# Order of rounding, drains and small statistics at four section changes, and whole 2 MB ring slots for projections with 4 or 8 k tiles

## The chip, the cores and the metric

The kernel runs on one core of a Trainium2 chip. The metric is the device time of one execution in microseconds. The five engines are TensorE (PE), VectorE (DVE), ScalarE (ACT), GpSimd (POOL) and SyncE (SP); each works through its own instructions in program order and waits at semaphores for the others.

## What is computed

The input is one sequence of 256 tokens with 2048 columns, fp32. It goes through an even layer (a gated causal convolution of 31 taps with layer norm and a pointwise projection, beside block attention of 8 heads), an odd layer (latent attention of 16 heads with an index score that keeps 64 keys per query), a mixer (gated delta rule and a short convolution), cross attention to 256 memory rows, and a feed-forward part with a 3-tap convolution. Each is a residual with an RMS norm in front. Nearly all time goes to projections. The change touches these parts of the reference:

```python
z = _rmsnorm(x, norm_g) @ w_in                      # even and odd layer
...
ya = _conformer_conv(...) * silu(a_gate)            # ends with y @ w_pw + b_pw      (e_pw)
x + jnp.concatenate([ya, yb], -1) @ w_out           #                                (e_out)
...
cq, ckv, ik, iw, gate = _split_cols(z, [512, 256, 64, 16, 2048])   # (o_small, o_gate0, o_gate1)
cq, ckv = _rmsnorm(cq, q_norm), _rmsnorm(ckv, kv_norm)
q  = cq @ w_qb                                      #                                (o_q)
iq = cq @ w_iq                                      #                                (o_iq)
ik = _layernorm(ik, ik_g, ik_b)
```

## The kernel before

**Tiling.** Every projection is a `Seg` (a section): `units` blocks of weights, `kt` k tiles of 128 rows. A narrow unit is 128 output columns for all k tiles, and its result is a [128, 256] tile in one of two PSUM banks. A wide unit (`e_out`, `o_out`, `f_down` and others) is a quarter of the k tiles for 512 output columns; four of them end a group of columns in PSUM for both halves of the tokens. Units are numbered through the whole kernel by `n0 + j`.

**Three products.** Weights and activations are each split in two fp32r parts, `hi` (the rounded value) and `lo` (the rest), and PE adds hi times hi, lo times hi and hi times lo. For each unit, ACT copies the weights of the ring slot to `w_hi` (`split`, L1090, wide L1087), DVE subtracts to get `w_lo` (L1604, wide L1600), PE multiplies (L604 and L605 for the paired sections, L607 to L609 for the others, L645 to L647 for the wide ones). The four buffers `whi`/`wlo` are used in turn, so a unit can be split once the unit four before it is done on PE. The activations lie in `h_cat`, written in rounds of four tiles: ACT writes the high part (`h_round`, L1267) and DVE the low part (`h_rest`, L1774).

**The ring.** SP loads weights into `RING = 2` slots of 2 MB. A chunk of the ring is two units, whatever `kt` is: 2 MB with 16 k tiles, 1 MB for `e_pw` with 8, 0.5 MB for `o_iq` and `o_q` with 4. The DMA for chunk c waits until every unit of chunk c - 2 is split.

**Order on ACT and DVE.** Behind the last matmul of a unit, ACT drains its PSUM bank (`drain`, for example L1104, L1124, L1138) and DVE does what follows (`post`: for paired sections L1637 adds the other half of the bank, then convolution taps or a product). Both lag three units behind the splits (`LAG = 3`). PE may write a bank again when the unit two before it is drained, or summed where the section is paired. `seg` runs a section: split unit j, drain or post unit j - 3. `section(name)` stands between two sections: it finishes all drains (or posts) of the section that ends and then splits four units of the next one. Inside `seg` a callback (`also` on PE, `late` on ACT) puts smaller work beside the units: `key_beside` in `o_gate0` (layer norm of the index key, transposes of the latent rows), `index_beside` in `o_gate1` (index scores of 16 heads).

**The statistics of `cq`, `ckv` and `ik`.** After `o_small` ACT squares `cq` and `ckv` (L1337, L1339), PE sums them over partitions with a matrix of ones (L749 to L752) before it begins `o_gate0`, ACT takes the roots (L1341, L1342) and DVE scales (L1892 to L1901).

**The feed-forward part.** It runs in three pieces, `f_up0` to `f_up2` (up projection, 3-tap convolution, SiLU, product on GpSimd at L553 to L557 into `act_cat`) and `f_down0` to `f_down2` (wide). On ACT the move from up to down has no `section`; on DVE it has `section(down.name)`.

Of the kernel before, what the change touches and what calls it, by code (L numbers as in the profile page):

```python
# [195 lines left out]
def build(nc, a, out):  # L196
# [149 lines left out]
    def p_tile(a_):  # L346
# [8 lines left out]
             "ht_hi", "ht_ready", "hhi_ready", "h_ready", "x_normed", "gain1_loaded", "gain_out_loaded",  # L355
# [41 lines left out]
    def chunk_src(g, c, k):  # L397

        cols2 = 2 * P
# [51 lines left out]
    def _(sp):  # L451
        sp.dma_start(x[:, 0, :], a["x"][0, 0:P]).then_inc(sem["x_loaded0"], 16)

        def load(g, i, b, looped):
# [15 lines left out]
            for cols, src in srcs:  # L470
                sp.dma_start(ring[slot][:, 0:g.kt, cols], src).then_inc(loaded[slot], 16)

        for g in order:
# [4 lines left out]
            for b in range(2):  # L478
                load(g, 0, b, False)
# [95 lines left out]
    def _(pe):  # L575
        mm = nc.tensor.matmul

        def unit(g, j, n, i=None, rhs=None, tiles_ready=None, norm=None):
# [13 lines left out]
            for k in range(g.kt):  # L592
# [21 lines left out]
        def seg(name, tiles_ready=None, rhs=None, also=None, norm=None):  # L614
# [3 lines left out]
            for j in range(g.units if straight else 4):  # L618
                unit(g, j, g.n0 + j, None, rhs, tiles_ready if j == 0 else None, norm if j == 0 else None)
# [130 lines left out]
        for t in range(CKT):  # L750
            mm(ps[3][:, 0:T], ones[:], osq[:, QT + t, :], start=(t == 0), stop=(t == CKT - 1))
        mm(ps[4][:, 0:T], ones[0:IDX_DIM, :], ik[0:IDX_DIM, :], start=True, stop=True).then_inc(sem["cq_stat"], 1)  # L752
# [31 lines left out]
        seg("o_gate1", also=index_beside)  # L784
# [279 lines left out]
    def _(act):  # L1064
# [10 lines left out]
        def split(g, j, n, i=None):  # L1075

            slot, m, kn = n % WHL, width(g, j), (n if i is None else n + 4 * i)
            c = g.c0 + (n - g.n0) // 2
# [10 lines left out]
            u0 = ((n - g.n0) % 2) * P  # L1089
            af(whi[slot][:, 0:g.kt, 0:m], ring[c % RING][:, 0:g.kt, u0:u0 + m], ACT.Copy).then_inc(sem["hi_ready"], 1)  # L1090
# [234 lines left out]
        section("e_out")  # L1325
# [10 lines left out]
        section("o_gate0")  # L1336
# [247 lines left out]
    def _(dve):  # L1584
# [7 lines left out]
        def split(g, j, n, i=None):  # L1592

            slot, m, kn = n % WHL, width(g, j), (n if i is None else n + 4 * i)
            c = g.c0 + (n - g.n0) // 2
# [7 lines left out]
            u0 = ((n - g.n0) % 2) * P  # L1603
            tt(wlo[slot][:, 0:g.kt, 0:m], ring[c % RING][:, 0:g.kt, u0:u0 + m],  # L1604
# [275 lines left out]
        section("e_out")  # L1880
# [8 lines left out]
        section("o_gate0")  # L1889
        dve.wait_ge(sem["cq_stat"], 1)  # L1890
        dve.wait_ge(*emptied(S["o_small"], 8))
        ch.link(nc.vector.tensor_scalar(ikt[:], ps[4][:, 0:T], 1.0 / IDX_DIM, None, ALU.mult))  # L1892
        ch.link(tt(ik[:], ik[:], ikt[:], ALU.subtract))
        tt(ikt[:], ik[:], ik[:], ALU.mult).then_inc(sem["ik_sq"], 1)
        dve.wait_ge(sem["cq_std"], 1)
        ch.link(nc.vector.reciprocal(orq[:], orq[:]))
        for t in range(CKT):
            ins = stt(ckv[:, t, :], ckv[:, t, :], col("kv_norm", t), orq[:, 1, :], ALU.mult, ALU.mult)
        ins.then_inc(sem["ckv_normed"], 1)
        for t in range(QT):  # L1900
            ins = stt(cq[:, t, :], cq[:, t, :], col("q_norm", t), orq[:, 0, :], ALU.mult, ALU.mult)  # L1901
        ins.then_inc(sem["cq_normed"], 1)
# [35 lines left out]
        section("o_q")  # L1938
# [291 lines left out]
```

## Time and profile before

| | |
|---|---|
| median of 3 runs | 2778.83 us (2774.16 to 2781.66) |
| profiled execution | 2779.45 us, span 2777.7 us, mean granted clock 0.966 |
| PE busy | 2553.9 us, 92% |
| DVE, ACT, GpSimd busy | 60%, 43%, 6% |
| DMA | 422.95 MB, mean 152 GB/s |

A line of the timeline gives the start in us, the duration in us, the engine, the line of code, the operation, output and inputs with shapes, and how many instructions of the same kind were merged (x4). In square brackets stands the idle time of the engine just before it, and what ended it. The granted clock is 1.00 at 2.4 GHz and 0.50 at 1.2 GHz; a number between them is a mean over a stretch with both.

### The profile page before, as it was taken

What the parts mean: (1) busy time and instruction counts of PE and PEld (TensorE: products, weight loads), DVE (VectorE), ACT (ScalarE), POOL (GpSimd) and SP (SyncE); (2) the same over time, 40 slices, a digit from 0 to 9 for tenths busy, and PEclk for the clock granted to TensorE, in tenths of its full rate; (3) what the DMA queues carried; (4) which work ended last, traced back from release to release, by engine and by line L of the source; (5) the groups of instructions that cost most, each with busy time, mean ns of one, the idle gap of its engine ahead of it and who ended that gap; (6) DMA issues with size and microseconds to landing.
All of it is one profiled execution on the core that took longest, in us unless ns stands there. A gap on an engine that the chain in (4) does not pass through costs nothing.

```text
span 2777.7 us, 36975 instructions
## 1 busy us (share of the span) xinstructions
PE 2553.9 (92%) x14778; PEld 2235.9 (80%) x14778; DVE 1664.3 (60%) x1948; ACT 1190.7 (43%) x1400; POOL 159.8 (6%) x136
## 2 busy tenths in 40 slices
PE   5999889988889999999886998998999999999998
PEld 5878877888777788988875887996788788878886
DVE  4799745534654577486446545443577647765764
ACT  5333754533454554543224535433455434433433
POOL 0000000000110010000000000000012202220220
PEclk9999999999999999999998999998999999999999
DMA  5544525444341555554005454543555555546544
GB/s 193 175 153 168 166 92 182 155 137 149 96 141 54 182 165 170 176 163 147 1 1 182 159 174 153 180 145 105 175 182 181 177 187 186 190 168 201 187 134 159
DMA packets 356310, 422.95 MB, mean 152 GB/s; under 512 B 14667, under 2 KB 293978, under 8 KB 355418
## 3 DMA queue, kind: packets, MB, share of 16 engines
q1 hardware_dynamic: 352848, 411.32, 45.4%
q0 software_dynamic: 2160, 8.40, 0.9%
q8 instruction: 93, 1.52, 0.2%
q10 hardware_dynamic: 1178, 1.45, 0.1%
q14 instruction: 31, 0.25, 0.0%
HBM read 419.05 MB, written 2.10 MB: 152 GB/s over the span
## 4 chain that ended last, share of the span: by engine, by line
PE 82%; DVE 13%; ACT 3%; issue 1%; DMA 1%; ACTq 0%; DVEq 0%
PE ps L604 24%; PE ps L605 12%; PE ps L645 7%; PE ps L646 7%; PE ps L647 7%; DVE conv L1809 4%; PE ps L607 4%; PE ps L608 4%; PE ps L609 4%; PE ps L846 3%; DVE w_lo L1604 3%; DVE w_lo L1600 2%; PE ps L602 1%; PE ps L601 1%; PE ps L600 1%; PE ps L667 1%
## 5 line engine op out<-in xcount | busy, mean ns | idle before, releaser
L604 PE MATMUL ps<-h_cat,w_hi 128*128 128x512 f32 x3200 | 1144.8, 402 | 34.1 <-DVE h_cat L1774 14.1
L605 PE MATMUL ps<-h_cat,w_lo 128*128 128x256 f32 x3200 | 901.5, 282 | 0.0
L1604 DVE TENSOR_TENSOR w_lo<-ring,w_hi 128x2048 fp32r<-128x2048 f32 (+2 forms) x298 | 628.2, 2112 | 355.2 <-ACT w_hi L1090 352.5
L604 PEld LDWEIGHTS ps<-h_cat,w_hi 128*128 128x128 f32 x3200 | 604.7, 189 | 191.3 <-DVE w_lo L1604 15.8
L605 PEld LDWEIGHTS ps<-h_cat,w_lo 128*128 128x128 f32 x3200 | 608.3, 190 | 2.0 <-issue 1.9
L1090 ACT ACTIVATE w_hi<-ring 128x2048 fp32r<-128x2048 f32 (+2 forms) x298 | 525.3, 1768 | 130.6 <-PE ps L647 64.1
L1600 DVE TENSOR_TENSOR w_lo<-ring,w_hi 128x2048 fp32r<-128x2048 f32 (+1 forms) x120 | 272.0, 2283 | 232.0 <-ACT w_hi L1087 232.0
L1087 ACT ACTIVATE w_hi<-ring 128x2048 fp32r<-128x2048 f32 (+1 forms) x120 | 221.1, 1855 | 325.2 <-PE ps L647 251.4
L607 PE MATMUL ps<-h_cat,w_hi 128*128 128x256 f32 (+2 forms) x928 | 267.8, 289 | 10.8 <-DVE w_lo L1604 10.1
L608 PE MATMUL ps<-h_cat,w_hi 128*128 128x256 f32 (+2 forms) x928 | 263.9, 284 | 0.0
L645 PE MATMUL ps<-w_hi,h_cat 128*128 128x512 f32 x576 | 228.9, 397 | 38.0 <-DVE h_cat L1774 33.4
L609 PE MATMUL ps<-h_cat,w_lo 128*128 128x256 f32 (+2 forms) x928 | 263.7, 284 | 0.0
L1104 ACT ACTIVATE stage<-ps 128x256 f32<-128x256 f32 x144 | 55.4, 385 | 430.4 <-PE ps L605 430.4
L646 PE MATMUL ps<-w_lo,h_cat 128*128 128x512 f32 x576 | 227.9, 396 | 0.0
L647 PE MATMUL ps<-w_hi,h_cat 128*128 128x512 f32 x576 | 227.5, 395 | 0.0
L607 PEld LDWEIGHTS ps<-h_cat,w_hi 128*128 128x128 f32 (+2 forms) x928 | 174.8, 188 | 16.3 <-DVE w_lo L1604 10.9
L608 PEld LDWEIGHTS ps<-h_cat,w_hi 128*128 128x128 f32 (+2 forms) x928 | 174.9, 189 | 1.3
L609 PEld LDWEIGHTS ps<-h_cat,w_lo 128*128 128x128 f32 (+2 forms) x928 | 174.8, 188 | 1.2
L645 PEld LDWEIGHTS ps<-w_hi,h_cat 128*128 128x128 f32 x576 | 110.6, 192 | 63.1 <-issue 34.9
L645 PE MATMUL ps<-w_hi,act_cat 128*128 128x512 f32 x352 | 139.6, 397 | 13.2 <-DVE w_lo L1600 13.2
L1637 DVE TENSOR_TENSOR stage<-stage,ps 128x256 f32<-128x256 f32 x144 | 60.4, 419 | 134.9 <-ACT stage L1104 134.3
L646 PE MATMUL ps<-w_lo,act_cat 128*128 128x512 f32 x352 | 138.8, 394 | 0.0
(382 smaller groups left out, 2976.5 us busy)
## 6 DMA issues: line engine op xcount, KB each, us to landing
ring<-in_w_ffn_up SPq DMA_DIRECT2D x44, 2048.0 KB, 8.0
ring<-in_even_w_in SPq DMA_DIRECT2D x28, 2048.0 KB, 8.0
ring<-in_w_mix_in SPq DMA_DIRECT2D x28, 2048.0 KB, 8.3
ring<-in_w_ffn_down SPq DMA_DIRECT2D x16, 2048.0 KB, 8.1
ring<-in_odd_w_in SPq DMA_DIRECT2D x11, 2048.0 KB, 8.4
ring<-in_even_w_out SPq DMA_DIRECT2D x8, 2048.0 KB, 8.1
ring<-in_odd_w_out SPq DMA_DIRECT2D x8, 2048.0 KB, 8.5
ring<-in_w_mix_out SPq DMA_DIRECT2D x8, 2048.0 KB, 8.1
```

The lines of the kernel that those rows point to most:

```text
L604: mm(o[:, 0:2 * T], whi[slot][:, k, :], flat(cat[:, k]), start=first, stop=False)
L605: ins = mm(o[:, T:2 * T], wlo[slot][:, k, :], cat[:, k, 0, :], start=False, stop=end)
L607: mm(o[:m, 0:T], whi[slot][:, k, 0:m], cat[:, k, 0, :], start=first, stop=False)
L608: mm(o[:m, 0:T], whi[slot][:, k, 0:m], cat[:, k, 1, :], start=False, stop=False)
L609: ins = mm(o[:m, 0:T], wlo[slot][:, k, 0:m], cat[:, k, 0, :], start=False, stop=end)
L645: mm(o[:], cat[:, k, 0, toks], hi, start=first, stop=False)
L646: mm(o[:], cat[:, k, 0, toks], lo, start=False, stop=False)
L647: ins = mm(o[:], cat[:, k, 1, toks], hi, start=False, stop=end)
L1087: af(flat(whi[slot])[:, 0:size], flat(ring[c % RING])[:, u0:u0 + size], ACT.Copy).then_inc(sem["hi_ready"], 1)
L1090: af(whi[slot][:, 0:g.kt, 0:m], ring[c % RING][:, 0:g.kt, u0:u0 + m], ACT.Copy).then_inc(sem["hi_ready"], 1)
L1600: tt(flat(wlo[slot])[:, 0:size], flat(ring[c % RING])[:, u0:u0 + size], flat(whi[slot])[:, 0:size].bitcast(F32), ALU.subtract).then_inc(se ...
L1604: tt(wlo[slot][:, 0:g.kt, 0:m], ring[c % RING][:, 0:g.kt, u0:u0 + m], whi[slot][:, 0:g.kt, 0:m].bitcast(F32), ALU.subtract).then_inc(sem[" ...
```

## The change

1. `per_chunk` replaces the fixed two units of a chunk: 4 for `e_pw`, 8 for `o_iq` and `o_q`, so that every chunk is 2 MB. `e_pw` and `o_q` have two chunks and `o_iq` one. ACT and DVE write these sections out unit by unit instead of looping.
2. `e_pw` to `e_out`: ACT and DVE split one unit of `e_out`, then finish the drains and posts of `e_pw`, then run the rounds of `ya` and `qe`; the further units of `e_out` are split inside `wide_seg`.
3. `o_small` to `o_gate0`: ACT splits two units ahead of the last drains of `o_small`. The statistics on PE run behind unit 0 of `o_gate0`, the roots on ACT and the scaling on DVE at j = 2; the variance of the key on PE moves from j = 1 to j = 2 and the transposes from j = 3 to j = 4.
4. `o_gate1` to `o_q`: a new semaphore `tiles_read` is raised when the last unit of `o_gate1` has issued its k tile 3. ACT splits two units, drains up to two units before the end, splits a third, waits for `tiles_read`, rounds `cq` into `h_cat`, and then drains the rest. DVE splits three units instead of four.
5. `f_up` to `f_down`: DVE's `section(down.name)` is dropped, so the splits of `f_down` and the last posts of `f_up` alternate.

```diff
+        self.per_chunk = 2 if wide else max(2, 2 * KT // kt)
...
-        g.chunks = (g.units + 1) // 2
+        g.chunks = (g.units + g.per_chunk - 1) // g.per_chunk
...
+    def chunk(slot, g):
+
+        n = g.per_chunk * P
+        return flat(ring[slot])[:, 0:g.kt * n].rearrange("p (k n) -> p k n", n=n)
...
-        ends[c] = g.n0 + min(2 * j + 2, g.units)
+        ends[c] = g.n0 + min(g.per_chunk * (j + 1), g.units)
...
+                if read is not None and k == QT - 1:
+                    ins.then_inc(sem[read], 1)
...
-        pe.wait_ge(sem["cq_sq"], 1)
-        for t in range(QT):
-            mm(ps[2][:, 0:T], ones[:], osq[:, t, :], start=(t == 0), stop=(t == QT - 1))
...
         def key_beside(j):
-            if j == 1:
+            if j == 0:
+                pe.wait_ge(sem["cq_sq"], 1)
+                for t in range(QT):
+                    mm(ps[2][:, 0:T], ones[:], osq[:, t, :], start=(t == 0), stop=(t == QT - 1))
...
+            if j == 2:
                 pe.wait_ge(sem["ik_sq"], 1)
...
-            if j == 3:
+            if j == 4:
                 pe.wait_ge(sem["ckv_normed"], 1)
...
-        seg("o_gate1", also=index_beside)
+        seg("o_gate1", also=index_beside, read="tiles_read")
```

The same on ACT:

```diff
-        section("e_out")
+        split_to(S["e_out"].n0 + 1)
+        drain_to(S["e_out"].n0)
         ya_round(1)
...
-        section("o_gate0")
+        split_to(S["o_gate0"].n0 + 2)
+        drain_to(S["o_gate0"].n0)
         af(osq[:, 0:QT], cq[:], ACT.Square)
...
-        act.wait_ge(sem["cq_stat"], 1)
-        af(orq[:, 0, :], ps[2][:, 0:T], ACT.Sqrt, bias=eps[:], scale=1.0 / Q_LORA)
-        af(orq[:, 1, :], ps[3][:, 0:T], ACT.Sqrt, bias=eps[:], scale=1.0 / KV_LORA).then_inc(sem["cq_std"], 1)
         def key_beside(i, b):
+            if 4 * i + b == 2:
+                act.wait_ge(sem["cq_stat"], 1)
+                af(orq[:, 0, :], ps[2][:, 0:T], ACT.Sqrt, bias=eps[:], scale=1.0 / Q_LORA)
+                af(orq[:, 1, :], ps[3][:, 0:T], ACT.Sqrt, bias=eps[:], scale=1.0 / KV_LORA).then_inc(sem["cq_std"], 1)
...
-        section("o_q")
-        act.wait_ge(sem["acc_ready"], S["o_gate1"].n0 + 8)
+        split_to(S["o_q"].n0 + 2)
+        drain_to(S["o_q"].n0 - 2)
+        split_to(S["o_q"].n0 + 3)
+        act.wait_ge(sem["tiles_read"], 1)
         h_round(H_GROUPS["cq_again"], 1, lambda q: cq[:], lambda q: None)
+        drain_to(S["o_q"].n0)
```

And on DVE, where the scaling of `cq`, `ckv` and `ik` (L1890 to L1902) also moves into `key_beside` at j = 2:

```diff
-        section("e_out")
+        split_to(S["e_out"].n0 + 1)
+        post_to(S["e_out"].n0)
...
-        section("o_q")
+        section("o_q", 3)
...
             seg(f"f_up{p}", links=8)
-            section(down.name)
```

## Rows read from the trace of the kernel before

**Rows 1.** The page, busy time of each engine, its share of the span, instructions.
```profile
PE 2553.9 (92%) x14778; PEld 2235.9 (80%) x14778; DVE 1664.3 (60%) x1948; ACT 1190.7 (43%) x1400; POOL 159.8 (6%) x136
```

**Rows 2.** Waits of PE: us in total, how many times, the longest.
```profile
PE ps L645 <- DVE w_lo L1600: 17.7, 4, 4.6
...
PE ps L604 <- DVE h_cat L1940: 3.8, 1, 3.8
```

**Rows 3.** Timeline of ACT, DVE and PE where `e_pw` ends and `e_out` begins.
```profile
443.02 7.30 ACT L1087 ACTIVATE w_hi<-ring 128x2048 fp32r<-128x2048 f32 x4
...
451.17 2.00 ACT L1267 ACTIVATE h_cat<-qe 128x1024 fp32r<-128x1024 f32 x2
...
444.95 8.90 DVE L1600 TENSOR_TENSOR w_lo<-ring,w_hi 128x2048 fp32r<-128x2048 f32 x4 [0.85 <-ACT w_hi L1087]
...
447.30 0.80 PE L645 MATMUL ps<-w_hi,h_cat 128*128 128x512 f32 x1 [4.60 <-DVE w_lo L1600]
...
455.69 0.39 PE L645 MATMUL ps<-w_hi,h_cat 128*128 128x512 f32 x1
```

**Rows 4.** Timeline where `o_small` ends; L731 is an earlier sum at full clock.
```profile
591.56 7.29 ACT L1090 ACTIVATE w_hi<-ring 128x2048 fp32r<-128x2048 f32 x4
...
600.37 3.52 PE L749 MATMUL ps<-osq,ones 128*128 128x256 f32 x8 [9.13 <-ACT osq L1339]
...
605.32 0.39 PE L607 MATMUL ps<-h_cat,w_hi 128*128 128x256 f32 x1
...
384.89 3.61 PE L731 MATMUL ps<-conv,ones 128*128 128x256 f32 x16
...
617.53 1.28 ACT L1347 ACT_TABLE_LOAD   x1
618.83 0.48 ACT L1347 ACTIVATE rstd<-ps,eps 128x256 f32<-128x256 f32 x1
```

**Rows 5.** Timeline of SP, ACT and PE where `o_iq` ends and `o_gate1` begins.
```profile
658.04 29.55 SPq L471 DMA_DIRECT2D ring<-in_odd_w_in  x4
...
667.41 1.91 ACT L1090 ACTIVATE w_hi<-ring 128x2048 fp32r<-128x2048 f32 x1 [6.40 <-DMA ring<-in_odd_w_in]
...
672.12 0.76 PE L604 MATMUL ps<-cq_cat,w_hi 128*128 128x512 f32 x1 [8.59 <-DVE iq L1637]
...
680.81 1.14 PE L778 MATMUL ps<-ik,iq 64*128 64x256 f32 x8
```

**Rows 6.** Timeline of DVE and ACT from the start of `o_q` to `o_out`.
```profile
730.99 2.50 DVE L1604 TENSOR_TENSOR w_lo<-ring,w_hi 128x512 fp32r<-128x512 f32 x4 [11.42 <-ACT w_hi L1090]
...
734.64 3.83 DVE L1927 SCALAR_TENSOR_TENSOR isum<-relu,iwt,isum 128x256 f32<-128x256 f32 x8
...
775.43 3.71 ACT L1087 ACTIVATE w_hi<-ring 128x2048 fp32r<-128x2048 f32 x2 [1.69 <-DMA ring<-in_odd_w_out]
```

**Rows 7.** DMA issues: count, KB each, median us from issue to landing.
```profile
ring<-in_odd_w_in SPq DMA_DIRECT2D x11, 2048.0 KB, 8.4
```

**Rows 8.** Windows: length, busy us of each engine, granted clock, DMA share, GB/s.
```profile
447.00:456.00 9.00, 8.70 (x26) 6.94 (x27) 9.00 (x6) 6.16 (x5) 0.00 (x0) 0.65 0.60 197
...
2196.00:2202.00 6.00, 5.85 (x16) 4.64 (x17) 6.00 (x4) 0.00 (x0) 5.64 (x3) 0.59 0.21 30
...
2471.00:2478.00 7.00, 6.83 (x24) 5.56 (x25) 7.00 (x4) 0.00 (x0) 6.64 (x3) 0.79 0.32 77
...
2699.00:2706.00 7.00, 6.48 (x22) 5.26 (x23) 7.00 (x4) 0.00 (x0) 6.08 (x3) 0.76 0.34 90
...
742.70:747.50 4.80, 4.76 (x18) 4.13 (x19) 4.59 (x14) 0.94 (x3) 0.00 (x0) 0.64 0.07 8
```

**Rows 9.** Timeline of DVE and POOL where `f_up0` ends and `f_down0` begins.
```profile
2186.40 0.42 DVE L1637 TENSOR_TENSOR stage<-stage,ps 128x256 f32<-128x256 f32 x1 [3.81 <-ACT stage L1104]
...
2193.81 11.49 DVE L1600 TENSOR_TENSOR w_lo<-ring,w_hi 128x2048 fp32r<-128x2048 f32 x4
...
2200.04 3.11 POOL L557 TENSOR_TENSOR act_cat<-fpr,act_cat 128x512 f32 x1 [0.19 <-POOL act_cat L556]
```

More of the change, by code:

```diff
@@ L397, in chunk_src @@
     def chunk_src(g, c, k):
-        cols2 = 2 * P
+        cols2 = g.per_chunk * P
         w1, w2 = a["even_w_in"][0], a["w_mix_in_2"][0]
@@ L470, in load @@
             for cols, src in srcs:
-                sp.dma_start(ring[slot][:, 0:g.kt, cols], src).then_inc(loaded[slot], 16)
+                sp.dma_start(chunk(slot, g)[:, :, cols], src).then_inc(loaded[slot], 16)
         for g in order:
@@ L477, in _ @@
                 continue
-            for b in range(2):
+            for b in range(min(2, g.chunks)):
                 load(g, 0, b, False)
@@ L576, in _, with unit @@
         mm = nc.tensor.matmul
-        def unit(g, j, n, i=None, rhs=None, tiles_ready=None, norm=None):
+        def unit(g, j, n, i=None, rhs=None, tiles_ready=None, norm=None, read=None):
             slot, m = n % WHL, width(g, j)
@@ L618, in seg @@
             for j in range(g.units if straight else 4):
-                unit(g, j, g.n0 + j, None, rhs, tiles_ready if j == 0 else None, norm if j == 0 else None)
+                unit(g, j, g.n0 + j, None, rhs, tiles_ready if j == 0 else None, norm if j == 0 else None,
+                     read if j == g.units - 1 else None)
                 if also:
@@ L745, in _ @@
         seg("o_small", norm=1)
-        pe.wait_ge(sem["cq_sq"], 1)
-        for t in range(QT):
-            mm(ps[2][:, 0:T], ones[:], osq[:, t, :], start=(t == 0), stop=(t == QT - 1))
-        for t in range(CKT):
-            mm(ps[3][:, 0:T], ones[:], osq[:, QT + t, :], start=(t == 0), stop=(t == CKT - 1))
-        mm(ps[4][:, 0:T], ones[0:IDX_DIM, :], ik[0:IDX_DIM, :], start=True, stop=True).then_inc(sem["cq_stat"], 1)
-        def key_beside(j):
-            if j == 1:
+        def key_beside(j):
+            if j == 0:
+                pe.wait_ge(sem["cq_sq"], 1)
+                for t in range(QT):
+                    mm(ps[2][:, 0:T], ones[:], osq[:, t, :], start=(t == 0), stop=(t == QT - 1))
+                for t in range(CKT):
+                    mm(ps[3][:, 0:T], ones[:], osq[:, QT + t, :], start=(t == 0), stop=(t == CKT - 1))
+                mm(ps[4][:, 0:T], ones[0:IDX_DIM, :], ik[0:IDX_DIM, :], start=True, stop=True).then_inc(sem["cq_stat"], 1)
+            if j == 2:
                 pe.wait_ge(sem["ik_sq"], 1)
                 mm(ps[5][:, 0:T], ones[0:IDX_DIM, :], ikt[0:IDX_DIM, :], start=True, stop=True).then_inc(sem["ik_var"], 1)
-            if j == 3:
+            if j == 4:
                 pe.wait_ge(sem["ckv_normed"], 1)
@@ L1088, in split @@
                 return
-            u0 = ((n - g.n0) % 2) * P
-            af(whi[slot][:, 0:g.kt, 0:m], ring[c % RING][:, 0:g.kt, u0:u0 + m], ACT.Copy).then_inc(sem["hi_ready"], 1)
+            u0 = ((n - g.n0) % g.per_chunk) * P
+            af(whi[slot][:, 0:g.kt, 0:m], chunk(c % RING, g)[:, :, u0:u0 + m], ACT.Copy).then_inc(sem["hi_ready"], 1)
         def drain(g, n, i=None):
@@ L1165, in seg @@
             g = S[name]
-            straight = g.units % 4 != 0 or g.name == "o_small" or unrolled
+            straight = g.units % 4 != 0 or g.name == "o_small" or unrolled or g.per_chunk > 2
             for j in range(g.units if straight else 4):
@@ L1602, in split @@
                 return
-            u0 = ((n - g.n0) % 2) * P
-            tt(wlo[slot][:, 0:g.kt, 0:m], ring[c % RING][:, 0:g.kt, u0:u0 + m],
+            u0 = ((n - g.n0) % g.per_chunk) * P
+            tt(wlo[slot][:, 0:g.kt, 0:m], chunk(c % RING, g)[:, :, u0:u0 + m],
                whi[slot][:, 0:g.kt, 0:m].bitcast(F32), ALU.subtract).then_inc(sem["lo_ready"], 1)
@@ L1679, in seg @@
             g = S[name]
-            straight = g.units % 4 != 0 or g.name == "o_small" or unrolled
+            straight = g.units % 4 != 0 or g.name == "o_small" or unrolled or g.per_chunk > 2
             for j in range(g.units if straight else 4):
@@ L1888, in _ @@
         seg("o_small")
[L1889 to L1902, printed above, removed]
-        def key_beside(i, b):
+        def key_beside(i, b):
+            if 4 * i + b == 2:
+                dve.wait_ge(sem["cq_stat"], 1)
+                dve.wait_ge(*emptied(S["o_small"], 8))
+                ch.link(nc.vector.tensor_scalar(ikt[:], ps[4][:, 0:T], 1.0 / IDX_DIM, None, ALU.mult))
+                ch.link(tt(ik[:], ik[:], ikt[:], ALU.subtract))
+                tt(ikt[:], ik[:], ik[:], ALU.mult).then_inc(sem["ik_sq"], 1)
+                dve.wait_ge(sem["cq_std"], 1)
+                ch.link(nc.vector.reciprocal(orq[:], orq[:]))
+                for t in range(CKT):
+                    ins = stt(ckv[:, t, :], ckv[:, t, :], col("kv_norm", t), orq[:, 1, :], ALU.mult, ALU.mult)
+                ins.then_inc(sem["ckv_normed"], 1)
+                for t in range(QT):
+                    ins = stt(cq[:, t, :], cq[:, t, :], col("q_norm", t), orq[:, 0, :], ALU.mult, ALU.mult)
+                ins.then_inc(sem["cq_normed"], 1)
             if 4 * i + b == 5:
```

8 lines of the change are left out of this document (4 added, 4 removed).

## The prediction

> **What bounds the kernel now.** I read the page first. TensorE (PE) is busy for 92% of the span [rows 1], so only two things can bring the end forward: less PE work, or less time in which PE stands or runs at the lower clock. The diff leaves PE's work as it is. Second I read the waits of PE, longest first. The reader should keep those whose releaser is a step that the diff moves: four stalls of a wide section's first matmul on its low halves, 17.7 us together, and 3.8 us ahead of `o_q` [rows 2]. Third comes the timeline around each stall, to see what stood ahead of the releasing instruction on its engine. In every one of these places PE waits for ScalarE (ACT) or VectorE (DVE), which work in program order, and they are late because of something that PE does not need yet. Fourth, the granted clock behind each stall: PE restarts at the lower level, so a stall costs more than its idle time [rows 8].
>
> **The change, place by place.** All times are of the profiled execution, 2779.45 us with a span of 2777.7 us; the median is 2778.83, so the sum stands 0.6 us above the median.
>
> *`e_pw` to `e_out`.* Now ACT rounds four units (443.02, 7.30 us) only behind the last drain, DVE makes their low halves (444.95, 8.90 us), and PE starts unit 0 at 447.30 after 4.60 us idle [rows 3]. The lower clock then stretches unit 0: 9.00 us at 0.65 cost 9.00 x 0.35 = 3.15 us [rows 8]. Unit 1 starts at 455.69 [rows 3]. The change splits unit 0 ahead of the last three drains. Its data is there, since the first `e_out` transfer then depends on the first 2 MB `e_pw` slot only, whose units were split before `e_pw` began. The cost: the sum of `e_pw` unit 5 on DVE waits for one low half, 8.90/4 = 2.2 us, and I find unit 7 of PE 0.4 us late. Unit 0 then starts at about 443.15 at full clock and ends at 448.6. But unit 1 is now split behind three rounds of `ya` and `qe`: about 444.5 + 1.0 + 2.0 (two rounds in 2.00 us [rows 3]) = 447.5, then 7.30/4 = 1.85 on ACT and 2.2 on DVE, so PE takes it at 451.75. Gain 455.69 - 451.75 = 3.9 us. What is late next is this new gap of 3.1 us, and the clock may fall again in it. Bounds: nothing, or the 3.15 us of [rows 8]. I take 1.5, near the 4.80 us x 0.36 = 1.7 us behind a short stall in `o_q` [rows 8]. Net 2.4.
>
> *`o_small` to `o_gate0`.* ACT splits four units (591.56, 7.29 us), then squares; PE idles 9.13 us, runs the statistics from 600.37 to 605.32, 4.95 us, much of it at the lower clock, and only then starts unit 0 [rows 4]. After the change two units are split during `o_small`. PE goes on from 591.1 with unit 0, 5.76 us (16 x 3 matmuls, 0.12 us apart, counted in the timeline), while ACT squares behind the last drain, 591.7 to 593.3. The statistics follow without a wait. At full clock eight such sums took 3.61 us [rows 4], so these seven take about 3.2. Unit 1 starts at 591.1 + 5.76 + 3.3 = 600.2 instead of 605.32 + 5.76 = 611.1: gain 10.9 us. The square root, the reciprocal and the scaling move to j = 2. Behind ACT's new wait for the statistics stand the split of unit 3 and the drain of unit 0. I get the drain at 604.8 and PE wants the bank at 606.0; DVE's low half of unit 3 ends at 609.8, wanted at 612.1. The root of the key variance moves from behind j = 1 to behind j = 2 on PE; the drain of unit 2 behind it ends at 617.5, wanted at 617.9. The tightest cover is thus 0.4 us.
>
> Here a rule speaks against the change. In the trace the table load before this root takes 1.28 us and the root starts as it ends (617.53 + 1.28 = 618.81, against 618.83) [rows 4]. The Trainium skill (ScalarE: Activation LUTs, What ACT_TABLE_LOAD costs) adds a drain of 1.38 us to every switch, 2.66 us in all. With two switches ahead of the drain of unit 2 the estimate by that page is 2.8 us later, 2.4 us past the cover, and a total 2.4 us higher. The rows leave no room for it, so the sum goes by them.
>
> *`o_iq` to `o_gate1`.* The small chunks make the first `o_gate1` transfer wait until unit 5 of `o_iq` is split: issued 658.04, and ACT takes unit 0 at 667.41 after 6.40 us idle. DVE stands behind that before it may add the halves of `o_iq` unit 5, so PE idles 8.59 us before unit 7 [rows 5]. With `o_iq` in one slot that transfer is free as soon as the last units of `o_gate0` are split, long before. What is late next: DVE still makes the low half of `o_gate1` unit 0 before it adds unit 5 (I get PE's unit 7 at 665.75), and that of unit 1 before it adds unit 6, so PE starts `o_gate1` at 668.45 and ends unit 0 at 674.2. The second chunk waits for the whole `o_iq` slot; issued at 660.95, with 8.4 us to landing [rows 7] and a split, the sum of `o_iq` unit 7 is done at 674.3, and PE's index product starts at 674.45 instead of 680.81 [rows 5]. Gain 6.35. The two short stalls left (2.4 and 1.3 us) may cost clock: 0 to 3.15, I take 1.4. Net 5.0.
>
> *`o_q` and `o_out`.* Rounding of `cq` starts once the last `o_gate1` unit has read its first four tiles, and one split less stands ahead. The 3.8 us stall [rows 2] goes, but PE soon waits for DVE, so DVE's queue counts. Its index sums start at 734.64 after four low halves from 730.99 [rows 6]; both they and the `cq` remainder now lie before ACT's last drain, and the sums start at 731.0. One low half returns inside `o_q` (2.50/4 = 0.6): 3.0 us earlier through `o_q`. Then ACT's splits of `o_out` units 2 and 3, started at 775.43 behind a DMA [rows 6], hold back the `qlat` copy. That transfer goes out 3.0 us earlier and is now alone, since the first `o_out` chunk left after eight units of `o_q`: 762.15 + 8.4 [rows 7] = 770.6. Gain 775.43 - 770.6 = 4.8 us for the two together.
>
> *`f_up` to `f_down`, three times.* DVE posts the last three `f_up` units and only then makes four low halves, 11.49 us beside GpSimd [rows 9]. ACT had rounded unit 0 long before. Without `section` unit 0's low half comes before the first of these posts, unit 1's and 2's between them, in time in which DVE idles (3.81 us before the post at 2186.40 [rows 9]). PE's stall goes: 17.7 - 4.6 = 13.1 us [rows 2], and with it the slow restart: 6.00 x 0.41 = 2.5, 7.00 x 0.21 = 1.5, 7.00 x 0.24 = 1.7 us [rows 8]. Sum 18.8. The next limit is GpSimd's last product, ready at 2200.04 + 3.11 = 2203.2 [rows 9]; PE would want it in unit 3, at about 2191.5 + 3 x 5.44 + 1.4 = 2209, so it stays covered (in the last part by some 3 us).
>
> These restarts differ after nearly equal stalls. The Trainium skill (TensorE: Matmul & The Clock Gate, What's actually happening) calls the number of slow matmuls run-variable, since it depends on where the first one falls. By that any single restart could come out 1 to 2 us either way; the sum keeps the measured ones.
>
> The wider slots cost nothing by themselves: PE's work and the bytes are the same, 2 MB lands in 8.4 us [rows 7], and each of these chunks is asked for more than that ahead of its first split.
>
> Sum: 2.4 + 10.9 + 5.0 + 4.8 + 18.8 = 41.9. 2779.45 - 41.9 = 2737.6, say 2738 us.
>
> **Rivals.** (a) The short stalls that stay cost no clock: 2.9 us more gain, 2735; if they cost all of 3.15 each, 2741. Both lie within my forecast. (b) The wide slots only move the wait: the second `o_gate1` chunk or the `o_out` chunk lands late (two 2 MB transfers in flight, as before 775.43), DVE stands in order behind it, and the gains of `o_iq` and `o_q` (9.8 us) go: 2748. For it: the chunk is asked for only when all of `o_iq` is split. Against it: 8.4 us to landing was counted already. (c) The `f_down` order gives nothing: a low half ahead of the sum of `f_up` unit 29 delays PE's last `f_up` units by what it saves later: 2756. Against it: DVE idles between those posts. (d) Slower: in `e_out` the change gives a burst of 5.4 us, a 3.1 us gap, and another start. If the lower clock held for the rest of that section, 15 units x 5.44 us = 81.6 us would double: 2738 + 82 = 2820. This decides from a loss of 42 us, that is 84 us at the lower level. Against it: no low stretch of [rows 8] lasts beyond 9 us. (e) The change does not do what it says, for instance because another releaser lies right behind each one: about 2775.
>
> **How the numbers follow.** Forecast with (a), 2731 to 2745: 0.68. Better than that: 0.06. (b) 0.12, (c) 0.07, (e) 0.04, (d) 0.03. The range for 8 in 10 is 2729 to 2751: it takes in (b) and part of what lies beneath. A measurement of this kernel can tell about 0.3% from no change, 8 us. Faster 0.94, same 0.03, slower 0.03.
>
> **What would show it.** PE without idle before the first matmul of each `f_down`, and the clock at 1.00 there; unit 0 of `o_gate0` right behind `o_small` and the statistics behind it without a wait; `e_out` with a gap of about 3 us between units 0 and 1; `o_gate1` unit 0 some 6 us earlier with ACT's DMA wait gone; the `qlat` copy 4.8 us closer to the end of `o_gate1`. Wrong would be: DVE waiting for a drain while PE waits for DVE in `f_up`, or a DMA wait of ACT in `o_gate1` longer than 5 us.

## The result and the profile after

The changed kernel takes 2734.84 us (median of 4 runs, 2732.40 to 2735.76) against 2779.05 us (median of 4 runs): a ratio of 0.9842, 95% interval 0.9825 to 0.9859, or 44.2 us less. The sum had given 2738, with 2729 to 2751 as its range. The profiled execution took 2735.5 us with a span of 2733.8 us at a granted clock of 0.972.

The page of the changed kernel answers to [rows 1]: busy time of each engine, its share of the span, instructions.

```profile
PE 2542.3 (93%) x14778; PEld 2228.4 (82%) x14778; DVE 1658.7 (61%) x1948; ACT 1190.4 (44%) x1400; POOL 151.2 (6%) x136
```

The counts are those of [rows 1]. PE is busy for 11.6 us less although it does the same work: most of that is time at the lower clock. The rest of the 43.9 us of span, 32.3 us, is idle time of PE. GpSimd (POOL) is busy for 8.6 us less, to which I come back.

The waits of PE after the change (us in total, how many, the longest) answer to [rows 2]:

```profile
PE ps L654 <- DVE w_lo L1615: 3.1, 1, 3.1
...
PE ps L610 <- DVE iq L1652: 2.2, 1, 2.2
...
PE ps L610 <- DVE qo L1652: 7.5, 9, 5.6
```

Before the change the last of these was

```profile
PE ps L604 <- DVE qo L1637: 4.7, 10, 2.5
```

Of four stalls at low halves one is left, 3.1 us. The 8.59 us of [rows 5] are 2.2 us. The 3.8 us ahead of `o_q` are gone, but PE waits 2.8 us longer in all for the sums of `qo`.

The timeline of PE in the changed kernel, each line with its idle time and releaser, shows the places one after the other:

```profile
450.89 0.50 PE L654 MATMUL ps<-w_hi,h_cat 128*128 128x512 f32 x1 [3.09 <-DVE w_lo L1615]
...
594.22 1.89 PE L760 MATMUL ps<-osq,ones 128*128 128x256 f32 x8
...
652.06 0.47 PE L610 MATMUL ps<-cq_cat,w_hi 128*128 128x512 f32 x1 [2.21 <-DVE iq L1652]
...
654.59 0.35 PE L613 MATMUL ps<-h_cat,w_hi 128*128 128x256 f32 x1 [0.89 <-DVE iq L1652]
...
660.50 1.14 PE L787 MATMUL ps<-ik,iq 64*128 64x256 f32 x8
...
755.26 2.05 PE L804 MATMUL ps<-qo,uk 128*128 128x256 f32 x4 [7.10 <-ACT qlat L1393]
```

The statistics (L760) follow unit 0 of `o_gate0` with no wait, where [rows 4] have 9.13 us. The gap in `e_out` is 3.09 us. `f_down` has no line here, because PE has no wait left at its start.

To see where the time went I took the start of the matmul that begins each stage in both traces and compared the distances. The last two columns compare two traces of one and the same changed kernel (the second from the experiments below) with the one trace behind the rows above.

| stage of PE | predicted gain | first trace | second trace |
|---|---|---|---|
| `e_pw` to the transposes of `o_small` (`e_out`) | 2.4 | 2.6 | 2.7 |
| to the first matmul of `o_iq` (`o_gate0`) | 10.9 | 10.5 | 10.5 |
| to the first index product (`o_iq`, `o_gate1`) | 5.0 | 6.8 | 4.2 |
| to the second `uk` product (`o_q`, `o_out`) | 4.8 | 4.2 | 5.0 |
| three starts of `f_down` and what follows in them | 18.8 | 19.0 | 19.1 |
| sum | 41.9 | 43.1 | 41.5 |

What is missing to the whole difference of span lies in stages that no edit touches: 0.8 us in the first trace; in the second 6.4 us, of which 3.2 around `x_out` (below). A table of all traces, further down, shows how far a stage differs between executions that leave it alone.

### The profile page after: what moved, and what is told of

Its sections match the earlier page's. It is cut to its first block, busy times and chain, and to the rows that moved or that the text cites. A ratio compares the mean times of both kernels' runs of the same rounds, so it can differ in the third digit from the quotient of the medians.

```text
span 2733.8 us, 36909 instructions
## 1 busy us (share of the span) xinstructions
PE 2542.3 (93%) x14778; PEld 2228.4 (82%) x14778; DVE 1658.7 (61%) x1948; ACT 1190.4 (44%) x1400; POOL 151.2 (6%) x136
## 4 chain that ended last, share of the span: by engine, by line
PE 83%; DVE 13%; ACT 2%; issue 1%; ACTq 0%; DMA 0%; DVEq 0%
PE ps L610 24%; PE ps L611 12%; PE ps L654 7%; PE ps L655 7%; PE ps L656 7%; DVE conv L1824 4%; PE ps L613 4%; PE ps L614 4%; PE ps L615 4%; PE ps L855 3%; DVE w_lo L1619 3%; DVE w_lo L1615 1%; PE ps L608 1%; PE ps L607 1%; PE ps L606 1%; PE ps L676 1%
## 5 line engine op out<-in xcount | busy, mean ns | idle before, releaser
L1615 DVE TENSOR_TENSOR w_lo<-ring,w_hi 128x2048 fp32r<-128x2048 f32 (+1 forms) x120 | 266.0, 2224 | 234.5 <-ACT w_hi L1096 234.5
L654 PE MATMUL ps<-w_hi,act_cat 128*128 128x512 f32 x352 | 137.0, 389 | 0.0
L656 PE MATMUL ps<-w_hi,act_cat 128*128 128x512 f32 x352 | 136.9, 389 | 0.0
```

The lines of the kernel that those rows point to most:

```text
L654: mm(o[:], cat[:, k, 0, toks], hi, start=first, stop=False)
L656: ins = mm(o[:], cat[:, k, 1, toks], hi, start=False, stop=end)
L1615: tt(flat(wlo[slot])[:, 0:size], flat(ring[c % RING])[:, u0:u0 + size], flat(whi[slot])[:, 0:size].bitcast(F32), ALU.subtract).then_inc(se ...
```

## The experiments

Two theories stood at the start. A: each stage's gain belongs to its own edit, and the gains add up. B: the edits lean on each other, the wide slots only move a wait, or releasers lie one behind the other, so that an edit alone gives little and the whole gives more than the parts. Four parts of the diff were run alone, then `o_q` alone, the whole without the slots, and extensions. Predicted prices are those of the sum.

**Slots of 2 MB alone.** The edit on top of the kernel before:

```diff
+        self.per_chunk = 2 if wide else max(2, 2 * KT // kt)
...
-        g.chunks = (g.units + 1) // 2
+        g.chunks = (g.units + g.per_chunk - 1) // g.per_chunk
```

> Kernel before with the 2 MB ring slots for e_pw, o_iq and o_q alone; every order on the engines as before. Theory A (each stall is an in-order queue of its own, the gains are local and add up): only the two waits for a DMA go. ACT's wait of 6.40 us before the first o_gate1 split goes and PE's stall before unit 7 of o_iq falls from 8.59 to about 2.2 us, 6.8 us with the restart at full clock; ACT's wait for the second o_out transfer falls by about 1.8 us. Sum 8.6 us, 2770. The stalls before e_out (4.6), o_gate0 (9.1), o_q (3.8) and the three f_down (13.1) stay as they are. Theory B (the slots are what makes the other orders pay, and by themselves do little): under 4 us, 2776 or more.

Measured: 2766.40 us against 2778.18 us (the median of 15 runs of the kernel before, made beside the four partial kernels), ratio 0.9960 (0.9948 to 0.9973). Timeline of PE in this kernel, the lines that answer to [rows 3] and [rows 5]:

```profile
446.80 0.80 PE L651 MATMUL ps<-w_hi,h_cat 128*128 128x512 f32 x1 [4.60 <-DVE w_lo L1606]
...
665.22 0.47 PE L610 MATMUL ps<-cq_cat,w_hi 128*128 128x512 f32 x1 [2.21 <-DVE iq L1643]
```

The stall in `e_out` is what it was; the one in `o_iq` went from 8.59 to 2.21 us, with no edit of the order. By the stages of this trace the slots give 6.75 us there and 1.9 us at the `o_out` transfer, 8.65 us for the 8.6 expected. The median fell by 11.8 us. The span of this trace is 14.0 us shorter, and 4.9 us of that lie between `o_out` and `x_out`, where the edit changes nothing; so the excess over 8.6 is not the slots' by anything that these runs show. Rival (b) of the prediction, that the wait only moves, is excluded, though not by much: the wide transfer does come late, and ACT waits 4.04 us for it. DVE stands behind ACT, and the sum of `o_iq` unit 7 behind DVE's low half. In the changed kernel (timeline of ACT, then DVE):

```profile
655.64 1.92 ACT L1099 ACTIVATE w_hi<-ring 128x2048 fp32r<-128x2048 f32 x1 [4.04 <-DMA ring<-in_odd_w_in]
...
659.80 0.41 DVE L1652 TENSOR_TENSOR iq<-iq,ps 128x256 f32<-128x256 f32 x1
```

That sum ends at 660.21. The index product, which needs it, starts at 660.50 without a wait: the cover is 0.3 us, and the prediction had it at 0.15.

**The `f_down` order alone.**

```diff
             seg(f"f_up{p}", links=8)
-            section(down.name)
```

> Kernel before with the section call on DVE between f_up and f_down dropped, three places, nothing else. Theory A: the three stalls of PE (4.56, 4.56, 4.03 us) go and with them the three restarts at the lower clock (2.5, 1.5, 1.7): 18.8 us, 2760. Theory C (the restart at the lower clock is not the stall's doing, or comes back elsewhere): the idle time alone, 13.1 us, 2766. GpSimd's last product, 9.3 us from start to end beside DVE's four low halves, should fall to about 5.5 us, since only one low half then lies beside it.

Measured: 2759.32 us, ratio 0.9928 (0.9911 to 0.9944), 18.9 us less. The three starts give 4.71 + 4.73 + 4.19 us, what follows each of them 2.36 + 1.37 + 1.61 us, 18.97 in all; in the changed kernel 4.74 + 4.72 + 4.20 and 2.37 + 1.37 + 1.60, 19.0. The interval of the ratio leaves out Theory C's 13.1 us (0.9953). Windows behind the start, the changed kernel at the first `f_down` and this one at the second (columns as in [rows 8]):

```profile
2166.00:2172.00 6.00, 6.00 (x29) 5.00 (x28) 4.02 (x6) 2.19 (x2) 3.00 (x1) 1.00 0.24 88
```

```profile
2471.00:2478.00 7.00, 7.00 (x32) 5.82 (x31) 3.73 (x2) 2.28 (x2) 0.81 (x1) 1.00 0.71 270
```

The clock is at 1.00 where [rows 8] have 0.59 and 0.79: PE does not stop, so it does not restart at the lower level. The prediction's 13.1 us of idle time and 5.7 us of clock measured 13.6 and 5.3 (by what lies ahead of the first matmul and behind it). Rival (c) is excluded. GpSimd's last work on `f_up0`, from the start of its first product to the end of its last, fell from 9.17 us (2193.98 to 2203.15) to 5.57 us (2198.30 to 2203.87), for the 9.3 and about 5.5 expected.

**The `o_gate0` order alone.** The splits of two units ahead of the last drain, the statistics behind unit 0, the root and the scaling at j = 2:

```diff
-        section("o_gate0")
+        split_to(S["o_gate0"].n0 + 2)
+        drain_to(S["o_gate0"].n0)
...
```

> Kernel before with the order at o_small to o_gate0 alone: two units split ahead of the last drains, the statistics behind unit 0, roots and scaling at j = 2. Theory A: idle 9.1 us and about 1.4 us of lower clock in the sums go, 10.5 us, 2768.5. Theory C: 9.1 us. If part of the gain comes from the stages around it (the clock of later stages, the ring), it is below 9 here.

Measured: 2766.80 us, ratio 0.9954 (0.9937 to 0.9970), 11.4 us less; its stage 10.9 us shorter. The total alone would also allow Theory C's 9.1 us (0.9967); the stage does not. PE has no wait in this stage. The tightest cover of the prediction, 0.4 us at the drain of unit 2, was 1.8 us in the changed kernel: the drain ended at 613.93 and PE took the bank for unit 4 at 615.72. The loads of ACT's tables there, back to the gate's behind each group of roots, and once to the root's (604.06), from ACT's timeline:

```profile
600.29 1.28 ACT L1133 ACT_TABLE_LOAD   x1
601.58 0.38 ACT L1133 ACTIVATE gate<-ps 128x256 f32<-128x256 f32 x1
...
604.06 1.28 ACT L1359 ACT_TABLE_LOAD   x1
...
612.26 1.28 ACT L1133 ACT_TABLE_LOAD   x1
613.55 0.38 ACT L1133 ACTIVATE gate<-ps 128x256 f32<-128x256 f32 x1
```

Each load takes 1.28 us, and the gate's activation starts 0.01 us later. The Trainium skill (ScalarE: Activation LUTs, What ACT_TABLE_LOAD costs) adds a drain of 1.38 us; these lines do not agree, and the 2.4 us of the estimate by that page did not come.

**The `e_out` order alone,** with the old slots.

```diff
-        section("e_out")
+        split_to(S["e_out"].n0 + 1)
+        drain_to(S["e_out"].n0)
...
```

> Kernel before with the order at e_pw to e_out alone, ring as before. Theory A: the first e_out transfer then leaves only after unit 5 of e_pw, lands at about 436.5 and delays the split by 1 us; PE's units 6 and 7 of e_pw come up to 1.3 us late, unit 1 of e_out waits behind the qe rounds, and the clock falls in that gap: 3.0 - 1.8 = 1.2 us gain. Theory B (without the slots the early split blocks the queue): DVE stands behind the transfer, e_pw's last sums are late by its whole landing time, a loss of 1 to 4 us.

Measured: 2779.73 us, ratio 1.0005 (0.9996 to 1.0015). Its stage is 1.8 us shorter in the trace, but the total does not show it: the next stage, which the edit doesn't touch, took 2.9 us more in this execution, with the same stall of 9.13 us in it. The interval even leaves out a gain of 1.8 us (0.9994). One trace cannot say whether the next stage gives it back in most executions or in this one alone; two other kernels that leave both stages alone pay the same 2.9 us there (below). What the trace does show is that Theory B's loss did not come.

**The `o_q` order alone.**

```diff
-        section("o_q")
-        act.wait_ge(sem["acc_ready"], S["o_gate1"].n0 + 8)
+        split_to(S["o_q"].n0 + 2)
+        drain_to(S["o_q"].n0 - 2)
+        split_to(S["o_q"].n0 + 3)
+        act.wait_ge(sem["tiles_read"], 1)
...
+        drain_to(S["o_q"].n0)
```

> Kernel before with the order at o_gate1 to o_q alone (tiles_read, three units split ahead), ring as before. Theory A: DVE's queue starts its index sums 3.6 us earlier and gets one low half back inside o_q, so 3.0 us less at the end of o_q; the second o_out transfer still lands 10 us after it is asked for, since two are in flight: 3.0 us in all. Theory B (needs the slots): below 1 us, with DMA waits of ACT in o_q that PE sees.

Measured: 2775.29 us, ratio 0.9987 (0.9978 to 0.9997), 2.6 us less than the 2777.91 us beside it; the trace gives 2.5 us in `o_q` and 0.3 behind it. So the split of the prediction's 4.8 us holds: order in `o_q`, slots at `o_out`.

**The whole without the slots.** `per_chunk` is 2 everywhere, all orders as changed.

> Kernel after without the 2 MB slots (all four orders, ring as before). Theory A: the slots are worth in it what they are worth alone, 8.6 us, and some 1 us more at e_out: 2734.8 + 9.6 = 2744. Theory B: the orders at e_out and o_q lose their gain too, another 7 us: 2751 or more.

Measured: 2745.04 us, ratio 0.9881 (0.9866 to 0.9896), 10.2 us more than the changed kernel in the first comparison, for the 9.6 of Theory A. By stages, the parts run alone sum to 1.8 (`e_out`) + 10.9 (`o_gate0`) + 2.8 (`o_q`) + 19.0 (`f_down`) + 0.5 + 6.75 + 1.9 (slots) = 43.6 us, the changed kernel has 43.1. (The 0.5 is the `e_out` stage in the trace of the slots, and within what that stage differs by itself.) The gains of the medians, 11.8 + 18.9 + 11.4 - 1.6 + 2.6, sum to 43.1 us, and the whole gave 44.2. They add up. Theory A stands, B falls.

**Closing the gap in `e_out`.** The prediction named what is late next: unit 1, split only behind three roundings of `ya` and `qe`. This kernel is the changed one with unit 1 split right behind the `ya` rounding, on ACT and, as below it, on DVE:

```diff
         ya_round(1)
+        split_to(S["e_out"].n0 + 2)
...
         h_rest(H_GROUPS["ya"], 1, ya[:, 4:8])
+        split_to(S["e_out"].n0 + 2)
```

> Kernel after with unit 1 of e_out split right behind the last round of ya and ahead of the two rounds of qe, on ACT and on DVE. Theory A: PE's gap of 3.09 us between units 0 and 1 of e_out falls to about 0.8 us, unit 1 at about 448.9 instead of 450.9, and, as no gap of 3 us is left, the clock stays at 1.00 in the section, where it cost 1.8 us: 3.9 us gain together, 2731. Theory C (the fall of the clock has to do with the short burst, not with the gap): 2.1 us gain, with the low stretch still there. Rival: the qe rounds now come later, and unit 2 waits for them: gap only moves, no gain.

Measured: 2730.33 us, ratio 0.9835 (0.9821 to 0.9848), 4.5 us less than the changed kernel's median for the 3.9 expected. PE in this kernel, and the window around it:

```profile
450.19 0.50 PE L654 MATMUL ps<-w_hi,h_cat 128*128 128x512 f32 x1 [1.18 <-DVE w_lo L1616]
```

```profile
440.00:460.00 20.00, 18.39 (x84) 15.01 (x84) 12.71 (x12) 10.75 (x9) 0.00 (x0) 1.00 0.47 155
```

The gap fell from 3.09 to 1.18 us and the clock stays at 1.00. In the changed kernel it did not; its window from 450 to 456 us, with the same columns:

```profile
450.00:456.00 6.00, 5.11 (x15) 4.07 (x16) 5.24 (x3) 2.12 (x2) 0.00 (x0) 0.72 0.66 201
```

That is 6.00 x 0.28 = 1.7 us of clock, close to the 1.5 of the prediction. The stage is 3.1 us shorter than in the changed kernel: 1.9 of idle time and most of the rest clock. It repeats: the stage takes 120.3 us in both traces of the changed kernel, and 117.0 to 117.2 us in the four traces of kernels with this edit. So Theory C, a fall of the clock by the short burst alone, is out.

**Closing the gap in `o_iq` too.** The first two splits of `o_gate1` go between the last drains of `o_iq`, and the posts likewise:

```diff
+        for j in range(2):
+            split_to(S["o_gate1"].n0 + j + 1)
+            drain_to(S["o_gate1"].n0 - 1 + j)
         seg("o_gate1", index_beside)
```

> The kernel before this one, and at o_iq to o_gate1 the sums of o_iq units 5, 6 and 7 are put on DVE (and their drains on ACT) between the first two splits of o_gate1 instead of behind them. Theory A: unit 7 of o_iq starts about 2 us earlier, o_gate1 about 1.8 us earlier, and its index product no longer waits for the sum behind the DMA of unit 2: 1.8 us more than the kernel before this one, 2729. Rival: the low half of o_gate1 unit 0 becomes what PE waits for and takes most of it: under 0.7 us.

Measured: 2725.85 us, ratio 0.9811 (0.9796 to 0.9826). The stall ahead of `o_iq` unit 7 went from 2.21 to 0.28 us, the 0.89 us ahead of `o_gate1` stayed, and the stage is 1.9 us shorter still, for the 1.8 expected. It is the same kernel as the third below.

**How much does one kernel differ from itself?** The kernel before, the changed one and the last were run again on another occasion.

> Kernel before once more, unchanged, for its trace. Theory A says that the small differences outside the edited places between the kernels so far (0.8 to 3.0 us, at o_gate0, o_out, g_out and the ends of f_down1 and f_down2) are the length of the low clock behind a stall that is itself the same length in each. Then the stalls of PE here are within 0.1 us of those of the first trace, and the time between two stalls differs by up to 3 us in some places, only where the granted clock differs. Rival: the places repeat to 0.1 us, and the differences belong to the edits.

> Kernel after once more, on the same chip as the next two, to compare with them: 2735 us, ratio 0.984.

> The kernel with both orders changed at e_out and at o_iq again, beside kernel after: by the places 3.1 + 1.9 = 5.0 us less than kernel after, 2730. The first runs gave 9.0 us less (2725.85), on another chip than kernel after. Rival: the 4 us above the places' sum are real and come back here, 2726.

Measured: 2778.03 us for the kernel before (one run); 2732.88 us, ratio 0.9830 (0.9815 to 0.9846), for the changed one; 2728.68 us, ratio 0.9820 (0.9806 to 0.9833), for the one with both gaps closed. The last two intervals overlap: both gaps closed are worth 4.2 us here and 9.0 by the medians of the earlier runs, against 3.1 + 1.9 us by the stages. That is small against the spread, but each of the two stages shows it.

Of the 39 stalls of PE above 0.8 us in the kernel before, 35 repeat within 0.1 us in its second trace, and the others differ by 0.1 to 0.55 us (the largest is the 8.59 us, now 8.04). The time between them does not repeat. The stages of the fourteen traces, in us, sorted by whether the kernel leaves the stage alone:

| stage of PE | left alone | as in the changed kernel |
|---|---|---|
| `e_out` | 122.2 to 123.0 (5 traces) | 120.3 (2) |
| `o_gate0` | 112.7 to 112.8 (3), 115.6 to 115.7 (3) | 102.2 to 102.4 (6) |
| `o_iq`, `o_gate1` | 27.1 to 28.0 (7) | 20.7 (3), 23.2 (1) |
| `o_q`, `o_out` | 98.5 to 99.5 (5) | 94.0 to 94.8 (6) |
| `f_up0` to the end | 771.6 to 775.0 (6) | 753.5 to 753.6 (8) |

Where the edit took a stall away altogether, the spread went with it: in `f_down`, and in the sums of `o_gate0`, which took 4.9 to 6.3 us and take 3.3 us in all eight traces with the edit. Where a stall is left, in `o_iq`, the spread is left too. By the extremes of the table the five places gain 38 to 51 us, and the trace behind the prediction lies at the low value of `o_gate0`. The second comparison of medians, 2779.81 against 2732.88, gives 46.9 us.

What mostly differs between two traces of one kernel is where the clock comes back. The changed kernel behind the stalls of 2.21 and 0.89 us in `o_iq`, first trace, then second; PE's timeline of the second ahead of its window:

```profile
655.00:660.00 5.00, 5.00 (x44) 5.00 (x43) 2.41 (x2) 2.18 (x2) 0.00 (x0) 1.00 0.99 310
```

```profile
651.45 0.47 PE L610 MATMUL ps<-cq_cat,w_hi 128*128 128x512 f32 x1 [2.21 <-DVE iq L1652]
...
653.99 0.55 PE L613 MATMUL ps<-h_cat,w_hi 128*128 128x256 f32 x1 [0.89 <-DVE iq L1652]
```

```profile
654.60:659.60 5.00, 5.00 (x25) 5.00 (x25) 2.52 (x2) 2.18 (x2) 0.00 (x0) 0.50 1.02 325
```

The stalls are equal to 0.01 us. In the first trace PE did 44 matmuls in 5 us at full clock, in the second 25 at half of it, and the stage took 2.5 us more. The first matmul of `x_out` behind equal stalls, again in the first trace and the second:

```profile
1887.21 0.76 PE L654 MATMUL ps<-w_hi,h_cat 128*128 128x512 f32 x1 [3.88 <-DVE h_cat L1789]
```

```profile
1884.27 0.47 PE L654 MATMUL ps<-w_hi,h_cat 128*128 128x512 f32 x1 [3.88 <-DVE h_cat L1789]
```

From the transposes behind `g_out` to those ahead of `f_up0` the first trace took 3.2 us more, 2.1 of it around this matmul. No edit touches that stretch.

The expectation for the kernel before, that traces differ only where the granted clock does, was missed at `f_up0`. There PE has no stall and the clock is at 1.00, and yet the stage was 3.3 us shorter in the second trace, evenly over its length. The same 20 us, first trace and second, in the columns of [rows 8]:

```profile
2040.00:2060.00 20.00, 20.00 (x116) 17.32 (x115) 15.39 (x19) 11.15 (x10) 2.74 (x3) 1.00 0.64 208
```

```profile
2040.00:2060.00 20.00, 20.00 (x118) 17.48 (x117) 15.89 (x18) 10.28 (x9) 3.36 (x2) 1.00 0.61 200
```

PE got through 118 matmuls instead of 116. The cause stays open.

**The same edit at `g_out` and `x_out`.** Two more wide sections were entered with four splits ahead of what PE waits for. On top of the last kernel, on DVE:

```diff
-        split_to(S["g_out"].n0 + WHL)
         for q in range(4):
+            split_to(S["g_out"].n0 + q + 1)
...
-        section("x_out")
+        post_to(S["x_out"].n0)
         for h in (2, 3):
+            split_to(S["x_out"].n0 + h - 1)
             x_drain(h)
         for q in range(4):
+            split_to(S["x_out"].n0 + q + 1)
```

> The same, and the lesson applied at two places that the change leaves alone, on DVE only. At g_out the four low halves (8.89 us) stand ahead of the low parts of the four activation rounds; they now alternate, and PE's stall of 26.5 us before g_out falls by 6.6 us. At x_out the four low halves stand ahead of the copy of head 2's output, for which PE waits 8.30 us; one low half now comes ahead of each of the two copies and the others between the rounds: PE's stalls of 8.30 and 3.88 us fall by 7 us together. Sum 13.6 us less than the kernel before this one, 2716. Rival: ACT's high parts, which keep their old order, become the bound and at least one of the two places gives under 2 us.

Measured: 2711.58 us (2708.04 to 2712.78), ratio 0.9757 (0.9744 to 0.9770): 2.4% below the kernel before, and the fastest of all. It fell by 17.1 us for the 13.6 expected. Timeline of PE, the first matmul of `g_out`, the values product before `x_out`, and `x_out`:

```profile
1438.68 0.77 PE L654 MATMUL ps<-w_hi,h_cat 128*128 128x512 f32 x1 [19.92 <-DVE h_cat L1793]
...
1853.26 3.69 PE L1034 MATMUL ps<-pe_pt,xv 128*128 128x256 f32 x16 [1.69 <-DVE xq L2172]
...
1860.83 0.47 PE L654 MATMUL ps<-w_hi,h_cat 128*128 128x512 f32 x1 [3.88 <-DVE h_cat L1793]
```

Before, these stalls were 26.5, 8.30 and 3.88 us. Each edit took away three of four low halves, 3 x 2.2 us = 6.6. The stall of 3.88 us did not fall. The span of the trace is 16.7 us shorter: 13.2 of it is idle time at these two places, the rest clock, nearly all of it from just ahead of the last line on, where the first matmul ran in 0.47 us instead of 0.76. Since the changed kernel did that too, in its second trace, this part cannot be put down to the edit.

## Why the prediction was right

**`e_out`.** 2.4 us predicted, 2.6 and 2.7 measured. The gap was taken at 3.1 us and is 3.09, and `e_pw`'s late unit at 0.4 us late and is 0.43. The two terms erred against each other: unit 1 starts 4.4 us earlier (455.69 - 450.89 - 0.38 gained ahead) where the sum had 3.9, and the clock cost 1.7 where it had 1.5. (The terms that the prediction adds for unit 1 give 451.55, and it writes 451.75.) Rival (d), the clock low to the end of the section, did not happen: the slow matmuls end by 455.8 us, 4.9 us after the restart, where the rival needed 84 us.

**`o_gate0`.** 10.9 against 10.5. The statistics, taken at 3.2 us, took from 594.22 to 597.52: 3.3 us. The agreement to 0.4 us has luck in it. In three of the six traces that leave this stage alone it takes 2.9 us more than in the trace behind the prediction, half of that in the sums themselves, and the difference to those is 13.4 us.

**`o_iq` and `o_gate1`.** 5.0 against 6.8 and 4.2. The mechanism and the instants were right: shifted by the 13.6 us gained ahead of it, the sum put PE's unit 7 at 652.2, `o_gate1` at 654.9 and the index product at 660.9; the trace has 652.06, 654.59 and 660.50. The term that was mis-sized is the clock behind the two short stalls, "0 to 3.15, I take 1.4". It was nothing in one trace and 2.5 us in the other. A single value for it is a mean of two outcomes, and the 5.0 lies between them by that choice.

**`o_q` and `o_out`.** 4.8 against 4.2 and 5.0. The 3.8 us wait went, and PE soon stood behind DVE, as predicted, at 719.37 for 5.57 us. DVE's index sums start 3.7 us closer to the index product, at 710.66, for the 3.6 of the sum. ACT's second pair of `o_out` splits still waits for its DMA, 0.80 us instead of 1.69:

```profile
750.92 3.71 ACT L1096 ACTIVATE w_hi<-ring 128x2048 fp32r<-128x2048 f32 x2 [0.80 <-DMA ring<-in_odd_w_out]
```

It came 24.5 us earlier than at 775.43 [rows 6], 20.3 of them gained ahead of `o_q`: 4.2 us for the 4.8 counted.

**`f_down`.** 18.8 against 19.0, the largest term and the best founded, since both the idle time and the clock were read from four rows of the same place. GpSimd's last product, the next limit, ended at 2174.57 us, 8.1 us behind PE's start of the section at 2166.45. PE wants it some 17.7 us behind that start by the prediction's count, and never waited for it. Against all six traces that leave these stages alone the gain is 18.0 to 21.5 us.

**The sum.** The 2737.6 us that it gave are 2.1 us above the profiled execution's 2735.5. The largest difference is the 1.8 us of `o_iq`, mostly its clock; 0.8 us lie outside the edited stages. No step of the mechanism failed, but that the total came within 2.1 us is in part chance: the stages as they were differ by up to 3.4 us each from one trace to another. The prediction allowed 1 to 2 us either way for a single restart, and 1.4 and 1.5 us were measured for two of them (below); the two in a row in `o_iq` gave 2.5 us together. Rivals (b), (c) and (e) are excluded by the runs of the slots, of `f_down`, and by all of them together. Of (a) both halves are true in turn: 4.2 or 6.8 us in the same place.

## What to carry to other kernels

On an engine that works in program order, put ahead of a drain or a sum that PE waits for only the one split that PE needs next, and the others between the drains; a call that makes all four units ready at a section change can cost PE the rounding of three units that it does not need yet. Here that was 6.6 us of idle time at `g_out` and ahead of `x_out`, with the restart 5.8 to 7.1 us at each `f_down` and 5.8 us at `e_out` once the next gap was closed too, and 10.5 us at `o_gate0`, where the sums moved as well. Cost such edits stage by stage from the timeline, since the parts added up within 1 us while the whole kernel's time could not show one of 1.8 us. And give the clock behind a stall two values, not one: the same kernel pays it in one execution and not in the next. A stall that is taken away altogether takes this spread with it.

## What was not expected of the hardware

**A restart's price is not set by its stall.** Behind the stall of 9.13 us the statistics took 4.95 us in the first trace of the kernel before [rows 4], and 4.9 in its second. In the kernel with the `f_down` order alone, where nothing near was edited, they took 6.3 us, from 601.86 to 608.16, and the whole stage 2.9 us more. The kernels with the `e_out` and the `o_q` order alone did the same. Timeline of PE in the first of these three:

```profile
601.86 3.78 PE L749 MATMUL ps<-osq,ones 128*128 128x256 f32 x8 [9.13 <-ACT osq L1339]
...
607.28 0.95 PE L752 MATMUL ps<-ik,ones 64*128 64x256 f32 x2
```

That is 1.4 us of the 2.9. The other 1.5 us lie at the start of `o_small`, behind a stall of 3.10 us that is the same in both. The same stretch in the kernel before, then in this one:

```profile
540.00:548.00 8.00, 6.63 (x55) 6.25 (x56) 6.33 (x16) 7.47 (x18) 0.00 (x0) 1.00 0.00 0
```

```profile
540.00:548.00 8.00, 7.47 (x42) 7.50 (x43) 5.44 (x14) 6.57 (x16) 0.00 (x0) 0.60 0.00 0
```

With 2.5 us in `o_iq` and 3.2 us around `x_out` this is the size of the spread of the runs, 3 to 12 us between the extremes of one kernel. What decides it within one kernel the runs don't show.

**The clock can fall after the restart.** Behind the gap of 3.09 us in `e_out` PE resumed with a first matmul of 0.50 us; the longer ones began at 452.45, 1.6 us later:

```profile
452.45 0.63 PE L654 MATMUL ps<-w_hi,h_cat 128*128 128x512 f32 x1
```

A first matmul at full clock is thus no sign that a gap was free.

**DVE's low halves and GpSimd's instructions take longer side by side.** In [rows 9] four low halves took 11.49 us, 2.87 each on average, and GpSimd's last product 3.11 us. With the low halves spread over `f_up` they took 2.29 us each, and GpSimd, in the changed kernel, did this:

```profile
2169.00 3.31 POOL L559 TENSOR_TENSOR fpr<-fsg,cvu 128x512 f32<-128x512 f32 x1 [16.37 <-DVE cvu L1638]
...
2172.48 0.61 POOL L562 CAST act_cat<-fpr 128x512 f32 x1 [0.17 <-POOL fpr L559]
...
2173.28 1.29 POOL L563 TENSOR_TENSOR act_cat<-fpr,act_cat 128x512 f32 x1 [0.19 <-POOL act_cat L562]
```

The same product took 1.29 instead of 3.11 us, and the cast ahead of it 0.61 instead of 2.44. It looks like taking turns. The first product is as long as before (3.26 us): in both traces it starts just behind a low half, which takes its 2.28 or 2.29 us undisturbed, and ends 1.15 us after it. The next low half of the kernel before, from 2196.02 beside GpSimd, took 3.37 us. GpSimd's 8.6 us and DVE's 5.6 us of busy time less on the page are of that size for three places; no run measured it by itself. Neither engine bounded the kernel here. But GpSimd's last product ended 3.6 us earlier than the prediction had it (2174.57 + 25.0 gained ahead of it = 2199.6, against 2203.2).
